# Background sums spread over a down step, and the main output stored by columns

## The reference

```python
for l in range(DEPTH):                     # DEPTH = 2
    sh1, sc1, g1, sh2, sc2, g2 = split(silu(cond) @ w_mod[l] + b_mod[l], 6)
    h = rms_norm(x, norm_mix[l]) * (1 + sc1) + sh1
    x = x + g1 * (attention(h) if l == 0 else conformer_conv(h))
    h = rms_norm(x, norm_ffn[l]) * (1 + sc2) + sh2
    x = x + g2 * ((silu(h @ w_gate[l]) * (h @ w_up[l])) @ w_down[l])
return x_prompt, x_sample, new_ckv, new_kpe   # x is (tokens, 1024)
```

## Time and profile before

| | |
|---|---|
| Runs | 1564.89 us median of 3 (1563.34 to 1567.29) |
| Profiled execution | 1563.13 us, its span 1561.3 us |
| Mean granted clock of TensorE | 0.996 |
| PE busy | 1526.1 us (98%) |
| DVE busy | 1154.8 us (74%) |
| ACT busy | 745.8 us (48%) |
| Chain that ended last | PE 81%, DVE 12%, ACT 4%, issue 2%, DMA 1% |

### The profile page before, as it was taken

The page is one execution under the profiler, slowest core; times in us unless marked ns, Lnnn a source line. Parts: engine busy times, 40 slices in busy tenths (PEclk is TensorE's granted clock), DMA queues, the critical chain, the costliest instruction groups (busy, mean ns, idle before and its releaser), DMA issues.

```text
span 1561.3 us, 26862 instructions
## 1 busy us (share of the span) xinstructions
PE 1526.1 (98%) x10707; PEld 1450.2 (93%) x10707; DVE 1154.8 (74%) x2125; ACT 745.8 (48%) x1367; POOL 140.5 (9%) x224
## 2 busy tenths in 40 slices
PE   8999999999999999999999999999999999999998
PEld 6989789799989989989999999989998999999998
DVE  5657877866886876787678999987788468568453
ACT  3445555553654244144235766775455335335332
POOL 0010111000011111111100023330001000000000
PEclk9999999999999999999999999999999999999999
DMA  9332332122244444533513389874314222222312
GB/s 331 109 109 61 110 104 82 37 81 82 82 136 149 137 147 140 184 109 129 176 61 95 75 181 178 180 143 109 109 55 156 89 81 75 89 81 75 96 63 78
DMA packets 141635, 178.15 MB, mean 114 GB/s; under 512 B 12961, under 2 KB 121193, under 8 KB 140488
## 3 DMA queue, kind: packets, MB, share of 16 engines
q1 hardware_dynamic: 120192, 109.68, 22.0%
q0 software_dynamic: 20992, 66.66, 16.7%
q10 hardware_dynamic: 328, 0.10, 0.0%
HBM read 148.93 MB, written 2.79 MB: 97 GB/s over the span
## 4 chain that ended last, share of the span: by engine, by line
PE 81%; DVE 12%; ACT 4%; issue 2%; DMA 1%; POOL 0%; ACTq 0%; DVEq 0%
PE PS L750 16%; PE PS L752 16%; PE PS L755 16%; PE PS L827 9%; PE PS L829 9%; PE PS L828 9%; PE PS L1145 1%; PE PS L884 1%; DVE WL L2022 1%; DVE PTL L2578 1%; DVE WL L1995 1%; DVE TMP L2187 1%; PE PS L1100 1%; DVE S L2012 1%; DVE X L2320 1%
## 5 line engine op out<-in xcount | busy, mean ns | idle before, releaser
L2320 DVE SCALAR_TENSOR_TENSOR X<-PS,MODV,X 128x128 f32<-128x128 f32 (+2 forms) x240 | 90.6, 434 | 167.0 <-PE PS L755 166.9
L827 PE MATMUL PS<-HH,WH 128*128 128x320 f32 x608 | 191.1, 314 | 8.9 <-ACT P L1730 8.2
L829 PE MATMUL PS<-HH,WL 128*128 128x320 f32 x608 | 187.9, 309 | 0.0
L828 PE MATMUL PS<-HL,WH 128*128 128x320 f32 x608 | 187.4, 308 | 0.0
L2022 DVE TENSOR_TENSOR WL<-RAW,WH 128x512 fp32r<-128x512 f32 x202 | 137.0, 687 | 48.5 <-ACT WH L1455 48.1
L1455 ACT ACTIVATE WH<-RAW 128x512 fp32r<-128x512 f32 x202 | 117.8, 621 | 104.6 <-PE PS L755 100.7
L750 PE MATMUL PS<-HIDH,WH 128*128 128x320 f32 x704 | 161.9, 310 | 0.7 <-DVE HIDL L2248 0.7
L755 PE MATMUL PS<-HIDH,WL 128*128 128x320 f32 x704 | 161.1, 309 | 0.0
L752 PE MATMUL PS<-HIDL,WH 128*128 128x320 f32 x704 | 161.0, 309 | 0.0
L1455 ACT ACTIVATE WH<-S 128x512 fp32r<-128x512 f32 x152 | 92.3, 623 | 105.2 <-DVE S L2012 105.2
L827 PEld LDWEIGHTS PS<-HH,WH 128*128 128x128 f32 x608 | 114.4, 188 | 26.5 <-issue 16.9
(11 more groups left out here) (409 smaller groups left out, 3587.8 us busy)
## 6 DMA issues: line engine op xcount, KB each, us to landing
RAW<-in_ffn_w_gate SPq DMA_DIRECT2D x22, 1024.0 KB, 5.2
RAW<-in_ffn_w_up SPq DMA_DIRECT2D x22, 1024.0 KB, 6.1
MODB<-in_w_mod POOLq DMA_DIRECT2D x72, 256.0 KB, 5.7
RAW<-in_ffn_w_down SPq DMA_DIRECT2D x24, 768.0 KB, 4.7
MODA<-in_w_mod POOLq DMA_DIRECT2D x48, 256.0 KB, 3.7
BGW<-in_w_mod POOLq DMA_DIRECT2D x24, 384.0 KB, 4.0
RAW<-in_conv_w_pw SPq DMA_DIRECT2D x16, 512.0 KB, 5.4
WL<-RAW POOLq DMA_DIRECT2D x8, 1024.0 KB, 10.0
```

The source lines that it names most:

```text
L827: mm(out, wh[:, c], xh(k), start=first and k == 0, stop=False, skip_group_check=True)
L828: mm(out, wh[:, c], xl(k), start=False, stop=False, skip_group_check=True)
L829: ins = mm(out, wl[:, c], xh(k), start=False, stop=k == HALF_K - 1, skip_group_check=True)
L2320: ins = V.scalar_tensor_tensor(out=X[:, m, t:t + b - a], in0=tile2(n)[:, bank, a:b], scalar=g, in1=X[:, m, t:t + b - a], op0=ALU.mult, op1 ...
```

## The change

The change has two independent parts.

1. BG_AT is changed so that the eight background tiles are done behind the channel tiles 1 to 5 of a down step instead of 1 to 7, and `part_turned` does one of the two BGACC at a time: the first behind channel tile 6, the second behind channel tile 7.
2. The main output is one array of shape (1024, 640), channels by tokens, which is the layout of X. SP stores X directly, in groups of the channel tiles 0 to 3, 4 and 5, 6, and 7 in two halves of tokens. The transposes on PE, the copies on ACT and YROWS are gone. The host transposes the array and splits it into the two outputs after the run.

```diff
-BG_AT = ((), (0, 1), (2,), (3,), (4,), (5,), (6,), (7,))
+BG_AT = ((), (0, 1), (2,), (3, 4), (5, 6), (7,), (), ())
+TURN_AT = (KT - 2, KT - 1)
...
-Y_GROUPS = ((0, 4), (4, 7), (7, 8))
+Y_GROUPS = ((0, 4), (4, 6), (6, 7), (7, 8))
...
+            y_tiles = y_columns.rearrange("(k p) t -> p k t", p=P)
             for a, b in Y_GROUPS[:-1]:
-                was_read(sp, ("y", b - 1))
-                ys = slice(a * P, b * P)
-                sp.dma_start(y_prompt[0][:, ys], YROWS[:, 0, ys]).then_inc(sem("y_stored"), 16)
-                sp.dma_start(by_tile[:, :, ys], YROWS[:, 1:QT, ys]).then_inc(sem("y_stored"), 16)
-            ys = slice(Y_GROUPS[-1][0] * P, D)
-            sp.wait_ge(sem("y_copied"), 1)
-            sp.dma_start(y_prompt[0][:, ys], YROWS[:, 0, ys]).then_inc(sem("y_stored"), 16)
-            sp.dma_start(by_tile[:, 0, ys], YROWS[:, 1, ys]).then_inc(sem("y_stored"), 16)
-            was_read(sp, ("y", KT - 1))
-            sp.dma_start(by_tile[:, 1:, ys], YROWS[:, 2:QT, ys]).then_inc(sem("y_stored"), 16)
+                was_read(sp, ("down", *LAST_DOWN, b - 1))
+                sp.dma_start(y_tiles[:, a:b, :], X[:, a:b, :]).then_inc(sem("y_stored"), 16)
+            sp.wait_ge(sem("x_half"), 1)
+            sp.dma_start(y_tiles[:, KT - 1, 0:HALF], X[:, KT - 1, 0:HALF]).then_inc(sem("y_stored"), 16)
+            was_read(sp, ("down", *LAST_DOWN, KT - 1))
+            sp.dma_start(y_tiles[:, KT - 1, HALF:TOK], X[:, KT - 1, HALF:TOK]).then_inc(sem("y_stored"), 16)
...
-                                    if (l, a) == LAST_DOWN and m + j and k == 2:
-                                        output_rows(m + j - 1)
...
-            def part_turned(q):
+            def part_turned(q, s):
                 dve.wait_ge(sem("bgw_used"), KT * (q + 1))
-                for s in range(2):
-                    link(V.transpose(PTURN[:].rearrange("p i g c -> p (i g c)"), BGACC[s][:]))
-                    ins = V.tensor_reduce(out=BGSUM[:, s, :, :], in_=PTURN[:], op=ALU.add, axis=mybir.AxisListType.X)
...
+                link(V.transpose(PTURN[:].rearrange("p i g c -> p (i g c)"), BGACC[s][:]))
+                ins = V.tensor_reduce(out=BGSUM[:, s, :, :], in_=PTURN[:], op=ALU.add, axis=mybir.AxisListType.X)
...
-                        if m == KT - 1:
-                            part_turned(chunk)
+                        if m in TURN_AT:
+                            part_turned(chunk, TURN_AT.index(m))
```

More of the change, by code:

```diff
@@ L167, in ffn @@
                 for m in range(1, KT):
-                    r += ([("y", m - 1)] if (l, a) == LAST_DOWN else []) + [("down", l, a, m)]
+                    r += [("down", l, a, m)]
         return r
@@ L174, in tile_order @@
     o += [("srow", "ln"), ("stat", "ln"), ("turn", "ln"), "mu", ("rb", "ln")] + [("pw2", m) for m in range(KT)] + ffn(1)
-    o += [("y", KT - 1)]
     return {n: i for i, n in enumerate(o)}
@@ L191, in program @@
             w_dq, q_norm, w_uq, w_dkv, kv_norm, w_ukv, q_hn, k_hn, w_o, w_pw1, b_pw1, w_dw, b_dw,
-            ln_g, ln_b, w_pw2, b_pw2, w_gate, w_up, w_down, y_prompt, y_sample, new_ckv, new_kpe):
+            ln_g, ln_b, w_pw2, b_pw2, w_gate, w_up, w_down, y_columns, new_ckv, new_kpe):
     T = tile_order()
@@ L305, in program @@
         LNROW = sb("LNROW", [P, 2, 3 * P], R_T[0])
-        YROWS = sb("YROWS", [P, QT, D], R_HH)
         HALF_K = KT // 2
@@ L618, in _ @@
                     sp.dma_start(new_kpe[0, 0], CKOUT[:, KVL:]).then_inc(sem("stored"), 16)
-            by_tile = y_sample[0].rearrange("(t p) d -> p t d", p=P)
+            y_tiles = y_columns.rearrange("(k p) t -> p k t", p=P)
             for a, b in Y_GROUPS[:-1]:
-                was_read(sp, ("y", b - 1))
-                ys = slice(a * P, b * P)
-                sp.dma_start(y_prompt[0][:, ys], YROWS[:, 0, ys]).then_inc(sem("y_stored"), 16)
-                sp.dma_start(by_tile[:, :, ys], YROWS[:, 1:QT, ys]).then_inc(sem("y_stored"), 16)
-            ys = slice(Y_GROUPS[-1][0] * P, D)
-            sp.wait_ge(sem("y_copied"), 1)
-            sp.dma_start(y_prompt[0][:, ys], YROWS[:, 0, ys]).then_inc(sem("y_stored"), 16)
-            sp.dma_start(by_tile[:, 0, ys], YROWS[:, 1, ys]).then_inc(sem("y_stored"), 16)
-            was_read(sp, ("y", KT - 1))
-            sp.dma_start(by_tile[:, 1:, ys], YROWS[:, 2:QT, ys]).then_inc(sem("y_stored"), 16)
+                was_read(sp, ("down", *LAST_DOWN, b - 1))
[4 more added lines that the diff above has]
+            sp.dma_start(y_tiles[:, KT - 1, HALF:TOK], X[:, KT - 1, HALF:TOK]).then_inc(sem("y_stored"), 16)
             sp.wait_ge(sem("stored"), 32)
-            sp.wait_ge(sem("y_stored"), 32 * len(Y_GROUPS) + 16)
+            sp.wait_ge(sem("y_stored"), 16 * (len(Y_GROUPS) + 1))
         @block.gpsimd
@@ L1316, in last_output @@
                         ins = split3([ps[:, i, 0:HALF]], wh, wl, [(HIDH[:, hs, t], HIDL[:, hs, t])], k == 0, k == n - 1)
[L1317 to L1324, removed]
                     ins.then_inc(mm_done if i else sem("down_half"), 1)
[L1326 to L1329, removed]
             ffn(0)
@@ L1844, in ffn @@
                                 gained("mix1", m, 1, 0)
[L1845 to L1861, removed]
             ffn(0)
@@ L1974, in _ @@
             ffn(1)
-            output_copy(KT - 1)
         @block.vector
@@ L2150, in part_tile @@
                     ins.then_inc(done, 1)
-            def part_turned(q):
+            def part_turned(q, s):
                 dve.wait_ge(sem("bgw_used"), KT * (q + 1))
-                for s in range(2):
-                    link(V.transpose(PTURN[:].rearrange("p i g c -> p (i g c)"), BGACC[s][:]))
-                    ins = V.tensor_reduce(out=BGSUM[:, s, :, :], in_=PTURN[:], op=ALU.add, axis=mybir.AxisListType.X)
[L2157 to L2160, removed]
+                link(V.transpose(PTURN[:].rearrange("p i g c -> p (i g c)"), BGACC[s][:]))
+                ins = V.tensor_reduce(out=BGSUM[:, s, :, :], in_=PTURN[:], op=ALU.add, axis=mybir.AxisListType.X)
+                if s:
+                    ins.then_inc(sem("bg_summed"), 1)
+                else:
+                    link(ins)
             def part_read(q, ps):
@@ L2822 @@
         "conv_b_pw2", "ffn_w_gate", "ffn_w_up", "ffn_w_down"]
-_OUTS = [((1, CTX, D), "float32"), ((1, LAT, D), "float32"), ((1, 1, CTX, KVL), "float32"), ((1, 1, CTX, ROPE), "float32")]
+_OUTS = [((D, TOK), "float32"), ((1, 1, CTX, KVL), "float32"), ((1, 1, CTX, ROPE), "float32")]
 def kernel(**inputs):
@@ L2840 @@
     r = run_bass_kernel_spmd(nc, [arrays], core_ids=[0])
-    return tuple(r.results[0][f"out_{i}"] for i in range(len(_OUTS)))
+    y, *new = [r.results[0][f"out_{i}"] for i in range(len(_OUTS))]
+    return (np.ascontiguousarray(y[:, :CTX].T)[None], np.ascontiguousarray(y[:, CTX:].T)[None], *new)
```

## The result

| | before | changed |
|---|---|---|
| Median | 1564.12 us of 4 runs (1562.69 to 1567.29) | 1549.13 us of 4 runs (1547.37 to 1549.55) |
| Span of the profiled execution | 1561.3 us | 1547.3 us |

The ratio is 0.9899 with a 95% interval of 0.9882 to 0.9917: 15.0 us less by the medians, for a predicted 1549.0 us. The time is that of the device alone: the transposition that the host now does after the run is not in it. Lines of the changed kernel are numbered a little lower: its fast matmuls are 822 to 824 instead of 827 to 829, `residual` is 2276 instead of 2320, `copied` 1704 instead of 1730.

The account below looks back on a forecast made before the run. PE, busy 98% of the span, was taken to bound the kernel, waiting on DVE's lateness behind down steps. −9.8 (sums) and −5.2 (output) made −15.0 us, giving 1549.0 us, range 1545.5 to 1553.5.

Parts of the forecast that it names:

- Rival (b): P5 waits behind down steps have another owner, reordering does nothing, only the output change gains: 1559 us; chance 0.05.
- Rival (d): Down steps: paired tiles leave DVE no idle, late background loads reach PE; slower, e.g. 1570 us at 18 us landing; chance 0.02.
- The sum of part 1: Gate steps behind down steps 0 to 2: moving background sums earlier removes PE's waits, −9.8 us.
- The course worked out for DVE: Down step 0 and gate: weight blocks start at 543.6, S2 at 547.0, P5 at 548.7, 1.3 us to spare.
- a tie: Behind down step 2: PE wants P5 at 803.5, there at 803.3; bounds nothing to 0.5 us wait, 0.1 taken.
- The low clock: Behind down step 0's wait: PE at 1.2 GHz costs 1.5 us more than step 1, taken as gone with the wait.
- rival (c): More than the sum: typical earlier runs lose low clock at two or three places, or stores end sooner; 1545 to 1546; chance 0.07.
- The sum of part 2: Output at the end: fewer PE matmuls (4.1) plus earlier last store (1.1) give −5.2 us.
- PE's 4.1: Last product matmuls: without 40 transposes PE needs 26.5 us instead of 30.59, 4.1 us gone, all on the path.
- The tail's 1.13: Behind the last matmul: last store issued 1.13 us earlier, its time to the span's end kept at 2.5 us.
- rival (a): Behind down steps 0 to 2: waits shrink but stay, 3.4 us given back, 1552.4 us; chance 0.15.
- two starting points 1.8 us apart: Profiled execution at 1563.13 us gives 1548.1, median of runs at 1564.89 gives 1549.9; forecast said 1549.0.

Follow-up runs that it names:

- The delay: Changed kernel with two more transposes and two more reductions on DVE before the second turn in down steps 0 to 2: 1563.94 us, ratio 0.9983 against the kernel before.
- the late turns: Changed kernel with both transposes and both reductions of the background sums behind channel tile 7 again: 1552.33 us, ratio 0.9916 against the kernel before.
- the sums only: Changed kernel with the whole old output (transposes, copies, YROWS, stores) put back, new background order kept: 1556.29 us, ratio 0.9940 against the kernel before.
- the transposes kept: Changed kernel with 35 of the 40 output transposes back on PE, ACT copying one column of each, stores unchanged: 1554.44 us, ratio 0.9932 against the kernel before.
- the one store: Changed kernel with channel tiles 0 to 6 stored in one 2.3 MB DMA instead of three: 1553.86 us, ratio 0.9921 against the kernel before.

## Why the prediction was right

**What bounds the kernel.** PE, and DVE through PE's waits behind the down steps. Two experiments show it. The delay makes DVE's weight blocks late again in the new order of tiles, by four operations more in front of them, and brings back the waits and takes the gain away; the late turns do it with nothing added, only in another place, and lose a part. Rival (b), another owner of the wait, is out. Rival (d) didn't happen: in the changed kernel DVE stands idle in front of none of its 48 passes over background tiles, though the tiles now come in pairs.

**The sum of part 1**, −9.8, was −9.6 by itself, and by the rows 10.0 at the three gate steps. The course worked out for DVE held to 0.1 us up to the weight blocks and S2: 3.48 us behind the start of the gate step, for 543.6 − 540.12 = 3.5, and S2 at 6.89 for 6.9. Copy and margin came out a little less well: P5 was free 8.92 us into the step where 8.6 was said, since ACT's copy now waits 0.24 us for PE's own product; so the margin is 1.03 us and not 1.3. Behind step 2, where I had called it a tie and put down 0.1 us, 0.2 us are to spare, and nothing was lost.

**The low clock** was taken as 1.5 us, once. The 1.5 is right as the difference of the stretches behind steps 0 and 1 (3.93 − 2.41); the prediction's "16 matmuls in 3.5 us" would give only 3.5 − 2.35 = 1.15, since two of the 16 only reach into that window: 14 start in it. That it would go with the wait was right in every kernel whose waits behind the down steps had gone or had shrunk (the changed one, and the runs with the sums only, the turns late, the transposes kept, the one store). That it stands once in an execution was only that execution's case: of five executions with the long waits, it followed behind step 0 in five, behind steps 1 and 2 in two each. The Trainium skill, page "TensorE: Matmul & The Clock Gate", Part 1, says that the gate's observation runs free and that the place of a transition varies; at steps 1 and 2 the traces agree, with one stretch in one profile and three in the next, at step 0 they show no variation. Three of the five have one stretch, as the execution that the prediction started from, and two have three; the mean is 1.8 stretches, 2.7 us instead of 1.5. So on some executions part 1 brings 3 us more than forecast. That is rival (c) for those executions; the median of the runs doesn't show it. The runs of before spread from 1562.7 to 1568.3 us and those of the changed kernel from 1547.4 to 1549.6. Whether the low clock makes the main part of this spread is not shown. One to three stretches fit its size. But of every run only the mean granted clock is on record, to three digits: over the 22 runs of before beside the experiments it is 0.994 to 0.998, and the longer ones tend to have the lower clock (correlation −0.5), though 1563.46 and 1567.68 us both stand at 0.997. And the clock varies in other places too: from 105 to 118 us its mean is 0.87 in the first profile of before and 0.74 in the two later ones.

**The sum of part 2**, −5.2, was −5.35 by itself. PE's 4.1 were 4.2: of the 40 transposes 37 stood in front of the last matmul, 0.115 us each (35 put back alone: 4.03, the same for each). The tail's 1.13 were 1.37: the issue of the last store came exactly as early as said, and the store itself was 0.25 us shorter than the 2.5 I had kept. The Trainium skill, page "DMA: Bandwidth & Descriptors", Anatomy of one DMA, gives 2.0 us plus bytes over 436 GB/s for DMAs on GpSimd's path. The stores here go out from SyncE, which the section does not cover and the prediction did not say. As an estimate by that rule the 160 KB would take 2.4 us and 1280 KB 5.0; measured were 1.8 and 4.7, and the measurement decides.

**The step that was least sure** was the margin in step 2, and behind it rival (a). With one turn one tile later it would have come true: the execution with the late turns lost 2.95 us, 1.65 of it behind step 2.

**What was luck.** The mechanism held and each term to 0.3 us, but that both sums come to 15.0 us and the time to 1549.13 for 1549.0 is closer than anything here can tell. The 1549.0 is a middle between two starting points 1.8 us apart. The kernel before had medians from 1564.12 to 1566.25 us, and in the two profiled executions the places of the change gained 15.6 us and the span 14.0.

No version that beats the changed kernel showed up in the runs. The waits that it removed were the only ones of background sums. Its margins of 0.2 and 1.03 us are enough in all four profiled executions with the new order and nothing made later (271.1 to 271.4 us of gates and steps). Behind the last matmul stand 3.2 us, of which 2.3 are the last store's.

## What to carry to other kernels

When the bounding engine waits right behind a stretch, look at what the late engine did in that whole stretch: here DVE was idle for 3.3 us between its updates and then 3.6 us late, and moving the same work forward cost nothing that the rows show and removed waits at three places. Count a wait of the matmul engine with what follows it: 2.13 us of standing still cost 2.4 us at full clock and 3.9 where the low clock followed, and how often it follows is to be counted over several profiles, not read from one. For an output, ask whether the layout that the kernel already holds can be stored as it is, and send what is ready early, so that the last small store finds an empty path. The transposition itself is then left to whoever reads the output, here the host.

## What the runs showed of the hardware

- With waits of 2.1 to 2.3 us of PE, a stretch of 12 to 13 matmuls at 1.2 GHz followed or not: behind step 0 in 5 of 5 executions, behind steps 1 and 2 in 2 of 5 each. Behind the one wait of 1.33 us (turns late) none followed, a single case. Why step 0 is always hit is open; no run was made for it.
- Two stores of 160 KB in 1280-byte pieces landed in 1.8 us, less than the shortest of the stores in the earlier trace rows; 1280 KB took 4.7 us and 2240 KB 7.3, so 960 KB more cost 2.6 us, about 380 GB/s. Issued 2.9 us behind the 2240 KB, 160 KB landed after 5.2 us.
- A 128x128 float32 transpose among matmuls cost PE 0.115 us, though its row shows 0.273.
